# Chunked RWKV scan with its state carried ahead of the inverse, half steps interleaved, and modulation sums moved to TensorE

## The reference

```python
def step(s, inp):
    w_t, k_t, v_t, kk_t, b_t = inp[:5]
    sa = jnp.einsum("bhvk,bhk->bhv", s, -kk_t)
    s = s * w_t[:, :, None, :] + sa[..., None] * b_t[:, :, None, :] + v_t[..., None] * k_t[:, :, None, :]
    y = jnp.einsum("bhvk,bhk->bhv", s, inp[5]) if readout else None
    return s, y
```

## Time and profile before

| | |
|---|---|
| median of three runs | 3100.59 us |
| profiled execution, its own time | 3106.15 us |
| its span | 3104.4 us |
| mean granted clock of TensorE | 0.897 |
| layer 0: projection | 62.7 to 239.6 us |
| layer 0: scan, eight steps | 298.2 to 648.3 us |
| layer 0: SwiGLU's matmuls | 758.9 to 1302.3 us |
| layer 1: scan, eight steps | 1508.9 to 1815.8 us |
| layer 1: experts, not touched | 1912 us to the end |
| busy TensorE / DVE / ACT / POOL | 2693.6 / 2035.0 / 1437.0 / 1463.6 us |

### The profile page before, as it was taken

How to read it: one execution, slowest core, us unless ns; L and a number is a source line. 1 busy time by engine, 2 the same in 40 slices (tenths; PEclk the granted TensorE clock), 3 DMA queues, 4 the chain that set the end, 5 groups by cost and what they waited for, 6 DMA issues and landing times.

```text
span 3104.4 us, 56153 instructions
## 1 busy us (share of the span) xinstructions
PE 2693.6 (87%) x22507; PEld 2153.6 (69%) x22507; DVE 2035.0 (66%) x2196; ACT 1437.0 (46%) x1971; POOL 1463.6 (47%) x698
## 2 busy tenths in 40 slices
PE   5895878878988989879678877999999999999998
PEld 3683766645777767667466666878778787787876
DVE  3987334454948483434643436888888888888886
ACT  2232333333221222144434334777767677676775
POOL 3343011122434343324411132877868778687785
PEclk9997667779999999989677688999999999999999
DMA  6530000021433343211000015999989999899994
GB/s 219 177 141 11 3 3 2 3 76 61 176 109 140 118 149 114 90 55 55 5 3 3 3 56 196 366 324 348 339 322 365 324 350 339 324 362 323 349 344 151
DMA packets 255372, 535.10 MB, mean 172 GB/s; under 512 B 9664, under 2 KB 83664, under 8 KB 250064
## 3 DMA queue, kind: packets, MB, share of 16 engines
q1 hardware_dynamic: 252048, 528.51, 48.0%
q10 hardware_dynamic: 3136, 3.85, 0.4%
HBM read 531.28 MB, written 1.05 MB: 171 GB/s over the span
## 4 chain that ended last, share of the span: by engine, by line
PE 46%; POOL 21%; issue 15%; DVE 14%; ACT 4%; DMA 1%; ACTq 0%; POOLq 0%; DVEq 0%; SPq 0%
POOL unit_lo L487 20%; PE bank L338 9%; PE bank L340 9%; PE bank L339 9%; DVE arena L329 4%; PE bank L1839 2%; PE bank L1783 2%; DVE arena L1446 2%; PE bank L1796 1%; PE bank L1752 1%; PE bank L1773 1%; PE bank L1815 1%; PE bank L1823 1%; PE bank L1856 1%; POOL w_lo L308 1%
## 5 line engine op out<-in xcount | busy, mean ns | idle before, releaser
L487 POOL TENSOR_TENSOR unit_lo<-arena,unit_hi 128x512 fp32r<-128x512 f32 x378 | 910.7, 2430 | 298.2 <-ACT unit_hi L475 298.0
L487 DVE TENSOR_TENSOR unit_lo<-arena,unit_hi 128x1536 fp32r<-128x1536 f32 x378 | 814.0, 2165 | 168.8 <-ACT unit_hi L475 168.4
L475 ACT ACTIVATE unit_hi<-arena 128x2048 fp32r<-128x2048 f32 x378 | 723.8, 1918 | 271.1 <-PE bank L340 271.1
L308 POOL TENSOR_TENSOR w_lo<-arena,w_hi 128x2048 fp32r<-128x2048 f32 x78 | 383.1, 4912 | 618.6 <-ACT w_hi L302 618.6
L338 PE MATMUL bank<-h_hi,w_hi 128*128 128x512 f32 (+1 forms) x1008 | 387.4, 384 | 53.7 <-DVE h_lo L1287 41.3
L338 PE MATMUL bank<-unit_hi,x_hi 128*128 128x512 f32 x1008 | 399.1, 396 | 13.6 <-POOL unit_lo L487 7.1
L340 PE MATMUL bank<-unit_hi,x_lo 128*128 128x512 f32 x1008 | 394.3, 391 | 0.0
L339 PE MATMUL bank<-unit_lo,x_hi 128*128 128x512 f32 x1008 | 393.3, 390 | 0.0
L340 PE MATMUL bank<-h_hi,w_lo 128*128 128x512 f32 (+1 forms) x1008 | 377.1, 374 | 0.0
L339 PE MATMUL bank<-h_lo,w_hi 128*128 128x512 f32 (+1 forms) x1008 | 374.8, 372 | 0.0
L329 DVE SCALAR_TENSOR_TENSOR arena<-arena,cs 128x2048 f32<-128x2048 f32 x80 | 299.1, 3779 | 7.8 <-DMA arena<-in_w_mod_dram 7.4
(11 more groups left out here) (313 smaller groups left out, 4032.8 us busy)
## 6 DMA issues: line engine op xcount, KB each, us to landing
arena<-in_moe_w_dram SPq DMA_DIRECT2D x378, 1024.0 KB, 5.1
arena<-in_w_mod_dram SPq DMA_DIRECT2D x48, 1024.0 KB, 5.5
arena<-in_ffn_w_dram SPq DMA_DIRECT2D x42, 1024.0 KB, 5.0
arena<-in_w_in_dram SPq DMA_DIRECT2D x26, 1024.0 KB, 5.4
arena<-in_w_out_dram SPq DMA_DIRECT2D x8, 1024.0 KB, 9.3
arena<-in_ctx_dram ACTq DMA_DIRECT2D x1, 1024.0 KB, 11.1
arena<-in_x_dram ACTq DMA_DIRECT2D x1, 1024.0 KB, 13.6
arena<-in_w_in_dram SPq DMA_DIRECT2D x2, 512.0 KB, 3.9
```

Source lines behind the costliest of these rows:

```text
L308: pool.tensor_tensor(lo, slot_view(splits[i][0]), hi, ALU.subtract).then_inc(sem("w_lo"), 1)
L475: act.activation(moe_split(j)[0], moe_slot(j), ACT.Copy).then_inc(sem("w_hi"), 1)
L487: eng.tensor_tensor(MWL[j % MSPLIT][:, cols], raw, MWH[j % MSPLIT][:, cols], ALU.subtract) \
```

## The change

**The scan in items.** A layer's scan is now 16 items, step times half, one after the other. TensorE builds the inverse of item `i`, and puts the tail of item `i - 1` and the scores, sums and transposes of item `i + 1` between its levels:

```diff
+                for i in range(SITEMS):
+                    level_x(i, 1)
+                    if i:
+                        solve(i - 1)
+                    level_u(i, 1)
+                    if i:
+                        read_values(i - 1)
+                    level_x(i, 2)
+                    if i:
+                        read_z(i - 1)
+                        state(i - 1)
+                    level_u(i, 2)
+                    level_x(i, 3)
+                    if i + 1 < SITEMS:
+                        scores(i + 1)
+                    level_u(i, 3)
+                    level_x(i, 4)
+                    if i + 1 < SITEMS:
+                        z_sum(i + 1)
+                    level_u(i, 4)
+                    level_x5(i)
+                    if i + 1 < SITEMS:
+                        turn_bk(i + 1)
+                    join32(i)
+                    level_x6(i)
+                    join64(i)
```

**The level.** The first product takes whole rows of blocks, 4 matmuls of 32 x 128 in place of 16 of 32 x 32, and ACT copies 128 x 512 in place of 128 x 128, of which the second product uses the diagonal part:

```diff
-                            for r in range(4):
-                                for i in range(4):
-                                    e = (i + r) % 4
-                                    ins = mm(ps[blk(e), b + i, part(0)], w["LM"][blk(i), k, e], w["T"][blk(i), e],
-                                             start=True, stop=True)
...
+                    for r in range(4):
+                        ins = mm(ps[:, b + r, 0:P], w["LM"][blk(r), k].rearrange("s e t -> s (e t)"),
+                                 w["T"][blk(r)].rearrange("s e t -> s (e t)"), start=True, stop=True)
+                    ins.then_inc(sem("pe_x"), 1)
...
+                    if k < 5:
+                        act.activation(w["XS"], ps[:, b:b + 4, 0:P], ACT.Copy)
```

**The state enters ahead of the inverse.** `z_sum` forms `ZI` = S2'V + (rates x state) before the levels of its item, `solve` applies the inverse to it once (4 matmuls of 128 x 64), and `read_values`, `read_z` and `state` use the solved `ZS`. `UW`, `GT`, `YW`, the matrix `MI` and their evictions go. The state `MC` is kept as blocks of 128 x 128. A half's next scores wait for its state:

```diff
+                    if st and reads_out(l, st - 1):
+                        pe.wait_ge(sem("y_done"), reads(l, i - 2))
+                    if st % 4:
+                        pe.wait_ge(sem("state_done"), updates[l, st - 1, q])
```

**The products of a step** go from DVE to POOL, a step ahead, except those of the first step; the scaled keys are kept twice (`BK`):

```diff
-                    nc.vector.tensor_tensor(BS, BV[:, d, :, tok], EX[:, 1], ALU.mult)
-                    nc.vector.tensor_tensor(KS, KDIR[:, d, :, tok], EX[:, 1], ALU.mult)
...
+                    nc.gpsimd.tensor_tensor(BK[:, st % 2, 0], BV[:, d, :, tok], EX[:, 1], ALU.mult)
+                    nc.gpsimd.tensor_tensor(BK[:, st % 2, 1], KDIR[:, d, :, tok], EX[:, 1], ALU.mult)
```

**The modulation sums** leave DVE. After the weight unit `key` TensorE does the unit's sum itself, in four groups of 32 columns of the array, and the semaphore that frees the slot is now TensorE's:

```diff
-                for stream in range(2):
-                    ins = nc.vector.scalar_tensor_tensor(out=ACC[:, stream], in0=slot_view(("acc", m, k))[:, 0, :],
-                                                         scalar=cs[:, 2 * k + stream:2 * k + stream + 1],
-                                                         in1=ACC[:, stream], op0=ALU.mult, op1=ALU.add)
...
+                    for q in range(4):
+                        ins = mm(bank[mod_bank[m]][32 * q:32 * q + 32, :], cs[:, 2 * k:2 * k + 32], wv[:, q],
+                                 start=(k == 0), stop=(k == KD - 1))
+                    ins.then_inc(sem("mod_mm"), 1)
```

The sums hold a bank of their own through the SwiGLU, so the w2 products go through three banks, not four:

```diff
-                                wait(pe, "ffn_acc", KD * g + m - 3)
...
+                                wait(pe, "ffn_acc", KD * g + m - 2)
```

More of the change, by code:

```diff
@@ L377, in hybrid_kernel, with reads @@
             YTOT.append(2 * yn)
+        SITEMS = 16
+        updates, un = {}, 0
+        for l_ in range(L):
+            for st_ in range(8):
+                for q_ in range(2):
+                    un += st_ % 4 != 3
+                    updates[l_, st_, q_] = un
+        UTOT = [updates[l_, 7, 1] for l_ in range(L)]
+        def reads(l, i):
+            return 2 * ybefore[l, i // 2] + i % 2 + 1
         def CTOK(l, ct):
@@ L968, in _ @@
+                zero_t(0)
+                masked_levels(0)
+                for i in range(SITEMS):
+                    if i == 0 or i in (7, 8):
+                        zero_t(i + 1)
+                    if i % 2 == 0 and i // 2 < 7:
+                        stage(i // 2 + 1)
+                    if i + 1 < SITEMS:
+                        masked_levels(i + 1)
+                    half(i)
                 rtok = LTOK(l)
@@ new lines, in _ @@
+                ins.then_inc(sem("staged"), 1)
+                masks(0, "S2")
+                masks(0, "S1")
+                first_t(0)
+                for i in range(SITEMS):
+                    if i:
+                        join64(i - 1)
+                    level_t(i, 1)
+                    level_t(i, 2)
+                    if i:
+                        read_out(i - 1)
+                        state(i - 1)
+                    if i >= 8 and i % 2 == 0:
+                        bonus(i // 2 - 4)
+                    level_t(i, 3)
+                    if i + 1 < SITEMS:
+                        masks(i + 1, "S2")
+                    level_t(i, 4)
+                    if i + 1 < SITEMS:
+                        masks(i + 1, "S1")
+                    full_t(i)
+                    if i + 1 < SITEMS:
+                        first_t(i + 1)
@@ L1519, in _ @@
+                join64(SITEMS - 1)
+                read_out(SITEMS - 1)
                 rtok = LTOK(l)
@@ new lines, in level_x5 @@
+                def level_x5(i):
+                    w, b = wk[i % 2], 4 * (i % 2)
+                    turn_t(i, 5)
+                    for r in range(4):
+                        for z, (f, g) in enumerate(pairs32(i // 8)):
+                            e = (2 * z + r) % 4
+                            ins = mm(ps[blk(e), b + f, part(5)], w["S1"][blk(f), 0, e % 2, e // 2, blk(g)],
+                                     w["T"][blk(f), e], start=True, stop=True)
+                    ins.then_inc(sem("pe_x"), 1)
@@ L1893, in _ @@
+                solve(SITEMS - 1)
+                read_values(SITEMS - 1)
+                read_z(SITEMS - 1)
                 rtok = LTOK(l)
                 pe.wait_ge(sem("y_done"), YTOT[l])
-                pe.wait_ge(sem("state_done"), 16 * (l + 1))
+                pe.wait_ge(sem("state_done"), UTOT[l])
                 for j in range(NP):
```

785 lines of the change are left out of this document (349 added, 436 removed).

## The result

The changed kernel takes **3205.47 us** (3205.24 to 3210.55), against 3100.63 in the same comparison: a ratio of 1.034, with a 95% interval of 1.032 to 1.036. It is slower by 105 us where 25 less was forecast, and beyond the range.

What follows compares the result with a forecast made beforehand. Bounds: half-clock small matmuls in the scans, waits for DVE in layer 0's SwiGLU. SwiGLU -49, projection -3, scan +28 sum to -24: 3082 us profiled, 3076 median. The forecast's own range was 3045 to 3112, the whole range 3000 to 3140.

Steps and rivals of the forecast that it cites:

- the half-speed share: Both scans: TensorE's clock at half speed for 30% of the time, giving 685 us; it was 57% before.
- the scan's term: Both scans together: 657.0 us before, 685 forecast, so +28, with bounds of -42 and +92.
- the tail: End of each scan item, 6 to 7 us of small matmuls, a third of an item, expected at half clock.
- through all levels: Old scan step: clock half from the middle of the next step's start through all levels, full through the dense products.
- The slower rival: Scans: the clock stays at half speed for 57% of the time, scans 749 us, total 3140; chance 0.18.
- The prices: Scan item: 19.2 us at full clock, 26.9 at half; without read-out 16.25 and 22.5; some 12.3 per layer uncovered.
- all at full clock: Both scans with the clock never at half speed: 615 us.
- The SwiGLU: Layer 0's SwiGLU: modulation sums leave DVE for TensorE, 543.4 us become 494; term -49, between -35 and -60.
- that rival: Modulation sums: a sum's four groups don't run side by side, 3.9 us instead of 0.985, total 3194; chance 0.05.
- The projection: Layer 0's projection: 16 new sums cost 15.8 us, a wait of 8.92 goes; term -3, between -15 and +10.
- POOL's products: Scans: rival that POOL's products hold DVE in every item they can, +20 us, total 3096; chance 0.10.
- The full-clock rival: Scans: the clock never falls, scans 615 us, -42, total 3006; chance 0.22.

Runs made afterwards that it cites:

- The pair of full and small products: The changed kernel plus 16 unused matmuls per item in TensorE's waits, with 128 x 128 tiles (full) or 32 x 32 (small): 3044.3 and 3271.1 us.
- the narrow level: The changed kernel with each level's first product as 16 matmuls of 32 x 32 and ACT copying 128 x 128: 3165.9 us; with 32 transposes per item, 3015.5.

## Why the prediction was wrong

**The step that failed** is the half-speed share: "I take half clock for 30% of the time, that tail or its equal: 615 + 70 = 685", with a bound of 57%, "the share of now". Measured were 82% and 92%, and the scan's term, +28, came out at +153. Everything hung on it, and the reason I gave, that "no wait of TensorE is longer than about 1 us by my chain, and dense pieces [...] come in each of the levels 1 to 4", read the clock by waits. The pair of full and small products shows that waits are not it: with small products in them, TensorE 94% busy, the clock stays at 0.64 and 0.56; with full ones it is 0.92 and 0.93. Nor was the tail the place: the clock falls ahead of it or in its first joins, and stays down through it and through levels 1 and 2. The longest regular wait was a little over my "about 1 us", once an item in the tail:

```profile
PE bank L1824 <- ACT arena L1153: 19.5, 16, 1.3
```

I had a row in hand that pointed the right way: in layer 0's third step the clock came back in an unbroken run of wide pieces, from `UW` at 419.88 through `GT`, `YW` and read-out, and was full at 425.0. The change takes `UW`, `GT` and `YW` out of that run and puts narrow levels between what is left of it. That this, of all that the change does, raised the share is argued; no run shows it by itself. What the runs show is that wide work put back brings the clock back.

**One step was taken for all.** The prediction has the old clock at half speed "through all levels". It read layer 0's third step. In the second and in four others of that layer the clock comes back ahead of the levels, behind the transposes and in the S2'V products that follow them, and the first level runs at full clock. The second step, and the third for comparison:

```profile
348.00:352.00 4.00, 2.79 (x14) 2.59 (x15) 2.77 (x6) 1.01 (x5) 1.02 (x2) 0.68 0.00 0
352.00:358.00 6.00, 4.93 (x187) 4.00 (x187) 0.58 (x2) 4.66 (x17) 0.00 (x0) 0.93 0.01 3
```

```profile
399.00:405.00 6.00, 4.86 (x249) 3.22 (x248) 0.86 (x3) 3.67 (x13) 0.00 (x0) 0.50 0.01 3
```

The same twelve transposes stand ahead of both, so the stretch at 395.0 was no sign for or against them. The experiments went against: with 32 transposes an item the clock was 0.95.

**The slower rival** had the sign and half the mechanism, short pieces between levels; the idling of TensorE that it put beside them is not it. Its size was too small: it priced the scans at 749 with the old share, +92, where +153 came. That share was a row of the kernel before taken for a limit of the kernel after, and the upper end of the range, 3140, came from it.

**The prices stand.** With the measured shares the item prices give 16 x (19.2 + 0.82 x 7.7) + 12.3 = 420 for layer 0 (measured 413.4), and for layer 1 8 x (19.2 + 0.92 x 7.7) + 8 x (16.25 + 0.92 x 6.25) + 12.3 = 399 (396.0). With 32 transposes an item, at a clock of 0.95, the scans take 324.5 + 302.8 = 627, where "all at full clock" was put at 615. In that kernel layer 0's items are 19.4 us apart on average, its 32 transposes included, against 19.2 by my chain.

**The SwiGLU**, forecast at 494 us, took 494.2. Waits of TensorE for DVE's additions are gone; the only ones left are for the normalized input, 12.7 us of the 13.8 ahead of the first matmul:

```profile
PE bank L313 <- DVE h_lo L1292: 13.8, 4, 12.7
```

and one sum takes 1.0 us, from 842.31 to the next matmul at 843.30, against 0.985 forecast:

```profile
842.31 1.06 PE L1648 MATMUL bank<-arena,cs 128*32 128x512 f32 x8
843.30 0.50 PE L313 MATMUL bank<-h_hi,w_hi 128*128 128x512 f32 x1
```

so the groups run side by side, and that rival falls. That the total fits so closely is partly luck. I had put 7 us on new waits, and TensorE was busy for 493.07 of the 494.20. What came in their place stands in part beside the sums: 0.33 us before this one and 0.34 from the next matmul to the one behind it, where 0.23 is the rule. **The projection** took 174.9 us, 2.0 less, where 3 were forecast; the other 3.0 of the 5.0 ahead of the first scan lie around it.

**POOL's products** held nobody. No wait of TensorE in the scans is for them, and DVE's product of state and decay takes the same time whether its first input is in SBUF or not, at most 295 ns:

```profile
L1479 DVE TENSOR_TENSOR arena<-arena,fac x32: 282/287/290, 381.6 to 1870.4; 64x128 f32<-64x128 f32 x32
L1479 DVE TENSOR_TENSOR arena<-bank,fac x16: 273/286/295, 332.1 to 1767.0; 64x128 f32<-64x128 f32 x16
```

The 20 us of that rival were 0. But by their starts and ends none of these 48 ran while any instruction of POOL did. So this says that they didn't meet, and not what would have happened if they had.

**The full-clock rival** was a kernel that doesn't exist by itself: it takes the added instructions to reach 0.95. With 32 transposes an item the change comes to 3025.1 us, and to 3015.5 with the narrow level, against the 3006 there.

## What to carry to other kernels

Before small matmuls are spread out or wide ones saved, read the granted clock beside the width of what ran, not beside the waits: a stage in which TensorE is 94% busy can run at half speed for most of its time all the same. When wide work is removed, don't take the half-speed share of the kernel before for a bound (here 57% became 82 and 92%). And where a wait has a free PSUM bank beside it, full-size transposes in it can cost less than the clock that they keep (here 1024 of them took 180 us off the change); too few don't hold it (512: 93 us), and five products an item on top of sixteen cost 26 us.

## What was not expected of the hardware

- TensorE's clock follows array use. Products of 32 x 32 and of 128 x 128, of the same length and in the same places, gave 0.64 and 0.92 in layer 0's scan, with TensorE busy for 94% and 91% of it.
- Transposes count. The Trainium skill (TensorE: Matmul & The Clock Gate, Part 4) has it that they don't count as TensorE being busy in the same way; here 32 of them an item held 0.95 and 0.95, more than 16 products of 128 x 128 did (0.92 and 0.93), where it was 0.59 and 0.54 without any. The measurement goes against the page.
- Where the clock is held for only part of the time, the same program is not steady: with 16 transposes an item seven executions of eight lay 1.2% apart (3095.6 to 3132.2 us), while the change itself, almost wholly at half speed, stayed within 0.2%.

Not tried, and open: what matmuls of a width between 32 x 32 and 128 x 128 do in these places, whether it is the load of 128 x 128 or the product that counts, and whether the pieces that the change removed would have held the clock had they been kept together in the new order.
